# Converting streamed weights two pieces at a time in a four-layer hybrid transformer kernel

## The reference

```python
h = rms_norm(x, norm_g)
z = h @ w_in                       # 1024 -> 6408
aq, ak, av, ag, mq, mk, mv, mi, mf, mo, mgate = split(z)
ya = sliding_window_sink_attention(rope(norm(aq)), rope(norm(ak)), av, sink) * silu(ag)
mq, mk = split(silu(causal_depthwise_conv(concat(mq, mk))))
hm = mlstm_chunkwise(mq, mk, mv, log_i, log_f)
ym = rms_norm(hm) * sigmoid(mo) * silu(mgate)
x = x + concat(ya, ym) @ w_out
```

```python
z = rmsnorm(x) @ w_in              # 1024 -> 13312
o_a = diff_attention(dq, dk, dv, lam, bias)
o_b = sum over groups of softmax(lse) * dilated_group(lq, lk, lv, window, dilation, bias)
o_m = memory_attention(mq, kv(mem))
merged = g0 * (f(o_a) @ w_br_diff) + g1 * (f(o_b) @ w_br_dil) + g2 * (f(o_m) @ w_br_mem)
x = x + merged @ w_out
```

## Time and profile before

| | us |
|---|---|
| median of three runs | 3065.07 (3063.97 to 3071.05) |
| the profiled execution | 3063.97 |
| its span, first to last instruction | 3062.1 |
| PE busy | 2944.4 |
| DVE busy | 1627.4 |
| ACT busy | 1263.0 |
| mean granted TensorE clock, of full speed | 0.987 |

### The profile page before, as it was taken

The page is one execution under the profiler, slowest core; times in us unless marked ns, Lnnn a source line. Parts: engine busy times, 40 slices in busy tenths (PEclk is TensorE's granted clock), DMA queues, the critical chain, the costliest instruction groups (busy, mean ns, idle before and its releaser), DMA issues.

```text
span 3062.1 us, 44919 instructions
## 1 busy us (share of the span) xinstructions
PE 2944.4 (96%) x18366; PEld 2566.3 (84%) x18366; DVE 1627.4 (53%) x3259; ACT 1263.0 (41%) x2640; POOL 188.4 (6%) x207
## 2 busy tenths in 40 slices
PE   8899999988999999999999999999999999999998
PEld 6888888988989889888888877887888888877886
DVE  6767645357674553677433554334677433564334
ACT  5555423255554232566333433223566333433222
POOL 3100000020000000200000000000200000000000
PEclk9899999999999999999999999999999999999999
DMA  3111322211113222322232222232322232222232
GB/s 114 45 52 58 104 69 63 83 52 51 58 51 106 75 79 80 114 84 79 76 117 90 76 76 69 96 97 97 114 81 77 81 115 92 76 76 76 93 100 76
DMA packets 99735, 250.24 MB, mean 82 GB/s; under 512 B 8597, under 2 KB 44845, under 8 KB 99274
## 3 DMA queue, kind: packets, MB, share of 16 engines
q1 hardware_dynamic: 99530, 247.37, 25.5%
HBM read 239.60 MB, written 6.50 MB: 80 GB/s over the span
## 4 chain that ended last, share of the span: by engine, by line
PE 79%; DVE 12%; ACT 5%; issue 2%; DMA 1%; POOL 1%; DVEq 0%; POOLq 0%; SPq 0%; ACTq 0%
PE ps L92 77%; PE ps L95 3%; ACT Z L98 2%; DVE Z L101 2%; DVE Z L109 2%; DVE ZR L101 2%; DVE cl L101 1%; ACT ch L98 1%; DVE Z L105 1%; DMA st<-in_stream_dram 1%; DVE Z L119 1%; DVE stat L122 1%; ACT ZR L98 1%; DVE stat L109 1%; ACT sq L98 1%
## 5 line engine op out<-in xcount | busy, mean ns | idle before, releaser
L101 DVE TENSOR_TENSOR cl<-st,ch 128x1024 fp32r<-128x1024 f32 (+1 forms) x436 | 500.4, 1156 | 635.5 <-ACT ch L98 635.0
L92 PE MATMUL ps<-hl,ch 128*128 128x264 f32 (+1 forms) x2816 | 834.8, 339 | 0.0
L92 PE MATMUL ps<-hh,ch 128*128 128x512 f32 (+1 forms) x2624 | 805.1, 347 | 24.9 <-ACT Z L98 11.5
L92 PE MATMUL ps<-hh,cl 128*128 128x512 f32 (+1 forms) x2624 | 795.5, 343 | 0.0
L98 ACT ACTIVATE ch<-st 128x1024 fp32r<-128x1024 f32 (+1 forms) x436 | 428.7, 990 | 509.5 <-PE ps L92 426.3
L92 PEld LDWEIGHTS ps<-hl,ch 128*128 128x128 f32 x2816 | 486.0, 190 | 59.6
L92 PEld LDWEIGHTS ps<-hh,ch 128*128 128x128 f32 x2624 | 454.5, 190 | 96.4 <-ACT Z L98 17.3
L92 PEld LDWEIGHTS ps<-hh,cl 128*128 128x128 f32 x2624 | 455.7, 190 | 59.3
L92 PE MATMUL ps<-ZR,ch 128*128 128x264 f32 (+2 forms) x1856 | 445.6, 337 | 5.5 <-DVE cl L101 5.1
L98 ACT ACTIVATE Z<-ps 64x128 f32<-64x128 f32 (+7 forms) x506 | 217.2, 437 | 436.9 <-PE ps L92 317.5
L92 PEld LDWEIGHTS ps<-ZR,ch 128*128 128x128 f32 x1856 | 304.9, 189 | 48.8 <-issue 12.8
(11 more groups left out here) (133 smaller groups left out, 3209.2 us busy)
## 6 DMA issues: line engine op xcount, KB each, us to landing
st<-in_stream_dram SPq DMA_DIRECT2D x372, 512.0 KB, 3.5
st<-in_stream_dram SPq DMA_DIRECT2D x64, 256.0 KB, 3.2
Z<-decay_rows SPq DMA_DIRECT2D x8, 904.0 KB, 6.6
Z<-bias_lines SPq DMA_DIRECT2D x16, 448.0 KB, 3.5
ya_spill<-Z SPq DMA_DIRECT2D x8, 512.0 KB, 4.5
Z<-ya_spill SPq DMA_DIRECT2D x2, 2048.0 KB, 7.7
Z<-in_x_dram SPq DMA_DIRECT2D x4, 512.0 KB, 5.3
Z<-in_mem_dram SPq DMA_DIRECT2D x2, 1024.0 KB, 5.7
```

What stands on the lines that cost most here:

```text
L92: return Ins(self, self.e and self.e.matmul(o, a, b, start=start, stop=stop, skip_group_check=True))
L101: return Ins(self, self.e and self.e.tensor_tensor(o, a, b, op))
```

## The change

The two pieces of the next unit are now converted one right behind the other, at the unit's last call, where before only the second one was. Nothing else is altered: the calls of `weights()` for units that are used in a single call, for the output projections, the branch products and the memory keys and values stand where they stood.

```diff
     def proj(self, key, nid, T, u, h, last=None):
         last = h == 1 if last is None else last
         self.put("proj", key, nid, T, u, h, last)
-        for _ in range(2 if last and not h else 1):
+        if last:
+            self.weights()
             self.weights()
 
     def projr(self, key, nid, u, h, k0=0, k1=8):
         self.put("projr", key, nid, u, h, k0, k1)
-        if k1 == 8:
+        if h and k1 == 8:
+            self.weights()
             self.weights()
 
...
                     put("mvmm", l, a, b, st["u"])
-                    if b in (1, 4):
+                    if b == 4:
+                        self.weights()
                         self.weights()
                     put("mvev", l, a, b)
...
                 put("dvmm", l, a, b, st["u"])
-                if b in (1, 3):
+                if b == 3:
+                    self.weights()
                     self.weights()
                 put("dvev", l, a, b, self.alt())
...
                         put("lvmm", l, c, a, u)
-                        if a in (1, 4):
+                        if a == 4:
+                            self.weights()
                             self.weights()
                         put("lvev", l, g, c, a, self.alt())
```

## The result

The changed kernel takes 3084.16 us (median of four runs, 3081.52 to 3089.0) where the kernel before takes 3065.49: the ratio is 1.0057, 95% interval 1.0046 to 1.0069. It is slower by some 17 us; 3072 was predicted, and the range ended at 3079. The profiled execution took 3080.72 us, its span is 3078.7 us.

A forecast was written before the change was run, and what follows sets the result against it. PE was taken as the bound, busy 2944.4 of 3062.1 us, so only its idle time or clock could change. Terms summed to +6.8 us on 3063.97, 3070.8; for a median 3072, range 3060 to 3079.

The forecast's parts named there:

- The steady case: Plain projections, most of the roughly 100 moved conversions: the first piece fits into an existing wait, so zero cost.
- rival 4: Transfers come late where single conversions closely follow a pair, up to 3.5 us each exposed; 3078, chance 0.04.
- Early attention: First two layers' attention, up to 134 us: DVE's lateness grows and stays, +3.7 us a layer, +7.4 in all.
- departures win nothing: Early attention: a conversion leaving DVE's list gains nothing, since the next DVE operation waits for work that PE delays.
- Ahead of 72 us: Three moved conversions there: one comes onto the path (+1.2), one leaves it (-1.2 to -2); 0 in all.
- Little slack: Unit starts near 168 and 229 us: 0.3 us each in the first layer, half that in the second; +0.9.
- the query evictions: Query evictions on ACT lose the copy ahead of them: gains of 0.2 us, four in all, -0.8.
- Gates: Gate projections at 320 us: a conversion leaves PE's 2.38 us wait and a clock dip probably goes; -4.7 for two layers.
- Group weights: At 1753 us the first conversion now stands behind ACT's `mqev` and PE waits 1.4 us; +2.6 for two layers.
- memory attention: Near 1839 and 1858 us moved conversions delay PE by 0.4 and 0.3 us; +1.4 for two layers.
- Rival 3: New waits at unit starts bring PE's clock down, each further dip costing 1.7 us on the path; 3081, chance 0.14.
- Rival 1: DVE's lateness is soaked up, its work being the same in sum; attention term 0 to 2, 3065, chance 0.22.

The follow-up runs named there:

- the wait filled: The changed kernel with 48 extra matmuls on PE ahead of the first convolution projection of each layer, results overwritten; ratio 1.0058.
- the run of the rest: The changed kernel with eight early-attention conversions (four in each of two layers) put back behind the first call; 3075.45 us, ratio 1.0028.
- the run of eight: The kernel before with only eight conversions moved, first pieces of the four units after the attention's start in each of two layers; 3078.47 us, ratio 1.0036.

## Why the prediction was wrong, step by step

**The steady case: right.** From 1507 to 1755 us PE is idle 2.7 us of 248, as before, and a transfer's lateness reaches PE at the same two places as before (1267 and 2189 us), for 2.8 us in sum and not 2.5. So rival 4 did not happen.

**Early attention: the mechanism right, the term too small.** Predicted +7.4 for two layers, measured 12.7. The steps in it, with DVE's lateness in the second layer's trace against the start of that layer: +1.1 and +2.9 at the first two returns (predicted 1.2 and 2.4), then +5.1 at the convolution (2.5, bounds 1.2 and 3.2). That step failed. Its working took 6.1 us for the call that starts at 100.1; in the first layer it started at 99.27 and took 7.8, in the second 8.0. Behind the wait of 6.83 us the clock stood at 0.50 for 3.4 us. A dip had stood there before too, but under the wait in the call's middle; the working left it out. With the wait filled the call took 5.8 us, 2.1 less, and DVE was 3.7 us late at this step in the second layer and 3.0 in the first, against 5.1 and 4.7. The 3.7 holds the 0.7 us by which the filler was too long; less that it is 3.0, within the bounds, by subtraction and not by a run. From there the steps come as predicted, +1.15 for each return, -1.15 for the departure (6.2, 5.1, 6.2). How DVE meets the late call, first layer:

```profile
108.81 0.69 DVE L101 TENSOR_TENSOR ZR<-ps,ZR 128x512 fp32r<-128x512 f32 x1 [2.40 <-ACT ZR L98]
```

One smaller slip in the same term: it said that the first unit is late "by about as much" as DVE's 1.2; its own numbers, 73.1 against 69.79, give 3.3, and 72.03, in a trace that is 1.1 us early there, is that. The argument that departures win nothing was right where the unit ahead had been made late too, as in the whole change, and not for single moves: those of 8, 72 and 76 each gave DVE 0.9 to 1.1 us.

**Ahead of 72 us: right.** 0; the run of the rest shows +1.1 for one piece, the run of eight -1.1 for the other.

**Little slack: half right.** The waits at the starts came (0.3 each), a third one near 293 us was not seen (+0.5), and the query evictions gave 0.3 to 0.4 each.

**Gates: the gain right, a loss beside it missed.** Moving 28 and 94 gives -2.7 us a layer, where 2.3 was said. But piece 26, moved with them, puts 1.03 us ahead of the attention step just in front, so idle time at the place sums to -0.1 a layer. What is left is the clock's part, -1.5 when it stays up and 0 when it doesn't: -3.1 in one execution and 0 in the other, against -4.7.

**Group weights and memory attention.** +2.6 predicted. PE's wait is 2.02 us, not 1.4, and the time +0.5 and +2.8, as the clock had it: 3.3. Memory attention +1.4 predicted, 1.7 + 0.9 measured, of which 1.0 is idle time.

**The sum.** 6.8 became about 17: 5 from the attention, 3 from the gates, 2 to 3 from the other places, and none of the errors had the other sign. Rival 3 named the right kind of price, a dip of the clock on the path, and had 0.14; but it counted on new dips, and the one that decided had been there all along, covered. Rival 1 is true of single moves at some places (8 and 76) and not at others (72).

## What to carry to other kernels

When the same amount of work is moved within a saturated engine's list, a single move can cost nothing, where it gives what it takes, or 2 us, where another engine's call starts late for it; and neighbouring ones cost more than their sum, here by about one conversion. Ask whether the lateness that one move gives another engine reaches back to where the next move was to pay. A wait that covers something else (a slow clock, a second wait) isn't free to grow or to move; price what it covers. Then place conversions one by one: two of these 130 moves gave 0.23%, all of them cost 0.57%.

## What the runs showed of the hardware

A wait of 1.25 us at one place left the granted clock at 1.00 in one execution and at 0.50 in another of the same kernel; each such stretch on the path cost 1.5 us, and the two profiled executions of the changed kernel had 16 and 19. While POOL ran a subtraction of 128x1024, 2.39 us, a DVE cast of 128x64 took 2.37 us and not 0.20.
